# The third branch's two units ahead of the dilated one in each group of the first attention

## The reference

```python
# A: six query heads, one key head; the keys are picked by an index score
logits = einsum(q, k_picked) * scale;  p = softmax(logits);  o_a = p @ v_picked

# B: dilated, three groups of four heads, (window, dilation) = (128, 1), (512, 4), (2048, 16)
pos = t - dil * arange(window // dil + 1)
e = exp(logits - m);  den = sum(e);  o = (e / den) @ v
lse = m + log(den);   alpha = softmax over the three groups of lse
o_b = sum over the groups of alpha * o

# C: window of 128, eight query heads on two key heads, a sink per head
m = maximum(max(logits), sink);  den = sum(exp(logits - m)) + exp(sink - m)
o_c = (exp(logits - m) / den) @ v

merged = g0 * (o_a @ w_a) + g1 * (o_b @ w_b) + g2 * (o_c @ w_c)
```

## Time and profile before

| | |
|---|---|
| median of 3 runs | 3436.84 us |
| the profiled execution | 3435.26 us |
| its span | 3433.5 us |
| PE busy | 3325.6 us, 97% |
| PE weight loads busy | 2738.0 us, 80% |
| DVE busy | 1700.4 us, 50% |
| ACT busy | 1338.7 us, 39% |
| POOL busy | 950.7 us, 28% |
| mean granted clock of PE | 0.982 |

### The profile page before, as it was taken

How to read it: one execution, slowest core, us unless ns; L and a number is a source line. 1 busy time by engine, 2 the same in 40 slices (tenths; PEclk the granted TensorE clock), 3 DMA queues, 4 the chain that set the end, 5 groups by cost and what they waited for, 6 DMA issues and landing times. The chain is left out here.

```text
span 3433.5 us, 55220 instructions
## 1 busy us (share of the span) xinstructions
PE 3325.6 (97%) x22824; PEld 2738.0 (80%) x22824; DVE 1700.4 (50%) x2672; ACT 1338.7 (39%) x2039; POOL 950.7 (28%) x629
## 2 busy tenths in 40 slices
PE   8999999999999999999999999899999999899998
PEld 7777887888778778878887859888887758898887
DVE  5886334313259753451413665554444566454454
ACT  5646333323255543332324362343324353343322
POOL 3325002444443420034443341241101342141100
PEclk9999999999999999999999999999999999999999
DMA  4200222222221022222232100212222200112222
GB/s 157 80 20 28 105 104 88 98 94 103 86 99 62 1 80 104 103 86 98 98 114 103 62 1 4 100 50 95 90 97 105 86 1 4 66 49 102 94 97 74
DMA packets 59684, 264.93 MB, mean 77 GB/s; under 512 B 13248, under 2 KB 27968, under 8 KB 30528
## 3 DMA queue, kind: packets, MB, share of 16 engines
q1 hardware_dynamic: 59456, 261.65, 21.8%
HBM read 259.53 MB, written 2.10 MB: 76 GB/s over the span
## 5 line engine op out<-in xcount | busy, mean ns | idle before, releaser
L1491 POOL TENSOR_TENSOR w_lo_f<-raw_f,w_hi_f 128x2048 fp32r<-128x2048 f32 x60 | 275.7, 4595 | 382.0 <-ACT w_hi_f L390 382.0
L402 PE MATMUL ps<-u_hi,w_hi_d 128*128 128x512 f32 (+1 forms) x768 | 291.5, 380 | 6.8 <-POOL u_lo L2929 5.6
L403 PE MATMUL ps<-u_lo,w_hi_d 128*128 128x512 f32 (+1 forms) x768 | 287.3, 374 | 0.0
L404 PE MATMUL ps<-u_hi,w_lo_d 128*128 128x512 f32 (+1 forms) x768 | 287.3, 374 | 0.0
L390 ACT ACTIVATE w_hi_f<-raw_f 128x2048 fp32r<-128x2048 f32 x64 | 121.9, 1908 | 253.8 <-PE ps L404 243.8
L402 PE MATMUL ps<-hid_hi,w_hi_f 128*128 128x512 f32 x512 | 199.2, 389 | 0.0
L403 PE MATMUL ps<-hid_lo,w_hi_f 128*128 128x512 f32 x512 | 199.2, 389 | 0.0
L404 PE MATMUL ps<-hid_hi,w_lo_f 128*128 128x512 f32 x512 | 199.2, 389 | 0.0
L1518 DVE TENSOR_TENSOR hid<-hid 128x512 f32<-128x512 f32 x64 | 119.0, 1860 | 139.6 <-ACT hid L1467 137.8
L656 POOL TENSOR_TENSOR w_lo_a<-raw_a,w_hi_a 128x2048 fp32r<-128x2048 f32 x28 | 129.0, 4609 | 199.7 <-ACT w_hi_a L652 199.7
L402 PEld LDWEIGHTS ps<-u_hi,w_hi_d 128*128 128x128 f32 x768 | 146.6, 191 | 35.4 <-POOL u_lo L2929 7.2
(11 more groups left out here) (463 smaller groups left out, 8585.0 us busy)
## 6 DMA issues: line engine op xcount, KB each, us to landing
raw_d<-in_w SPq DMA_DIRECT2D x70, 1024.0 KB, 4.8
raw_f<-in_w SPq DMA_DIRECT2D x64, 1024.0 KB, 4.8
raw_c<-in_w SPq DMA_DIRECT2D x40, 1088.0 KB, 5.0
raw_a<-in_w SPq DMA_DIRECT2D x22, 1024.0 KB, 4.9
raw_p<-in_w SPq DMA_DIRECT2D x22, 1024.0 KB, 4.8
raw_a<-in_w SPq DMA_DIRECT2D x18, 512.0 KB, 4.9
wo_raw<-in_w SPq DMA_DIRECT2D x4, 1024.0 KB, 6.3
h<-in_x SPq DMA_DIRECT2D x8, 256.0 KB, 4.3
```

Of the source, the lines that this page charges most:

```text
L402: nc.tensor.matmul(out, w_hi, x_hi, start=start, stop=False)
L403: nc.tensor.matmul(out, w_hi, x_lo, start=False, stop=False)
L404: return nc.tensor.matmul(out, w_lo, x_hi, start=False, stop=stop)
L1491: nc.gpsimd.tensor_tensor(WF[2][:, k % 2, :], WF[0][:, k % 2, :], WF[1][:, k % 2, :].bitcast(F32), ALU.subtract).then_inc(S["w_lo"], 1)
```

## The change

The list `units` is put together in another order: in each of the eight groups the two C units come first, then the B unit, then the A units as before. All else is derived from the list, on every engine.

```diff
             units = []
             for i, unit in enumerate(b_units):
-                units += [unit, *c_units[2 * i:2 * i + 2], *a_units[3 * i // 2:3 * (i + 1) // 2]]
+                units += [*c_units[2 * i:2 * i + 2], unit, *a_units[3 * i // 2:3 * (i + 1) // 2]]
```

## The result

The changed kernel takes 3442.57 us (median of 20 runs, 3438.04 to 3445.92), the kernel before beside it 3435.69 us (median of 20, 3434.57 to 3439.12). The ratio is 1.0017 with a 95% interval of 1.0011 to 1.0023: slower by 3.8 to 7.9 us, by 5.8 in the middle. The forecast was 3434.1, in a range of 3430.5 to 3438.9. The profiled execution took 3444.3 us with a span of 3442.5; it was one of the longer ones. One execution of an experiment, `act_copy_late`, took 7471.31 us; it is a slow run that nothing here explains, and it is left out of that experiment's ratio.

The account below looks back on a forecast made before the run. PE's (TensorE's) summed work bounds the kernel, so only its stalls and low clock can pay. Per attention 0.9 + 0.4 - 0.25 + 0.3 = 1.35 us, for two 2.7: 3436.84 - 2.7 = 3434.1 us, range 3430.5 to 3438.9.

Parts of the forecast that it names:

- The start: First units of each attention: PE's one idle of 3.0 us becomes three short ones; 0.9 us gained, bounds 0 and 1.6.
- first rival: The clock stays low through the start, B0's turn all low: 0.9 us less gained per attention, 3435.9 us; chance 0.18.
- The stall at 245.43: PE's stall early in the stage, before a C unit's values, goes: 0.4 us gained per attention.
- new wait of 0.25 before the turn of B1: At B1, the chain from logits to `wide` outlasts PE's work between: about 0.25 us lost per attention.
- The stalls after short B steps: Stalls in the steps after B2, B4, B6: 1.00 and 0.56 stay, 0.3 left of 0.56; gain 0.3 us per attention.
- The queues: Attention's end: slab transfers come later, ACT waits 1.0 us, hidden from PE with 0.6 us to spare.
- third rival: Slab 3 us later than counted: ACT's wait delays C15's copy and last exponentials, 2.4 us per attention, 3438.9; chance 0.12.

Follow-up runs that it names:

- act_copy_late: Changed kernel with ACT's wait for the slab and its copy one step later, in step 36; 3434.3 us, ratio 0.9992 to before; again 3435.34, 0.9998.
- copies_first: Changed kernel with DVE copying the turned B7 out of PSUM ahead of `o_lo` in step 36; 3434.1 us, ratio 0.9996 to the kernel before.
- last_group_only: Kernel before with only the last of the eight groups in the new order; 3445.8 us, ratio 1.0024 to the kernel before.
- before_act_late: Kernel before, old order, with ACT's wait and copy of the slab moved to step 36; 3436.15 us, ratio 0.9999 to the kernel before.
- last_group_old: Changed kernel with the last group back in the old order, first seven groups in the new; 3436.58 us, ratio 0.9996 to the kernel before.
- before_late_fetch: Kernel before, old order, with SP's slab transfers held back until the logits of C15; 3437.12 us, ratio 1.0005 to the kernel before.

## Why the prediction was wrong

**The start: right in kind, too large.** The chain was close: I had the turn of C0 at 4.16 us after PE's start, it was at 4.33; that of C1 at 6.86, it was 6.78; that of B0 at 8.9, it was 8.84. The waits for `sc` are there:

```profile
232.83 0.69 PE L1009 MATMUL ps<-cst,sc 128*128 128x128 f32 x2 [1.10 <-POOL sc L1094]
...
235.28 0.69 PE L1009 MATMUL ps<-cst,sc 128*128 128x128 f32 x2 [1.04 <-POOL sc L1094]
...
237.34 4.35 PE L1006 MATMUL ps<-wide,sc 128*128 128x128 f32 x24
```

The clock was where I had it, or somewhat later; what I had wrong is the price of the turn. I let the clock come back 11.0 us after PE's start. In the first attention it came back at 240.3, 11.8 us after the start, and in the second at 1144.8, 11.2 after it, each time in the midst of the first dilated turn:

```profile
240.00:241.00 1.00, 1.00 (x10) 1.00 (x9) 0.31 (x2) 0.00 (x0) 0.00 (x0) 0.84 0.00 0
...
1136.00:1137.00 1.00, 1.00 (x12) 1.00 (x9) 0.81 (x4) 1.00 (x7) 0.32 (x1) 0.50 0.00 0
...
1139.00:1140.00 1.00, 0.34 (x4) 0.05 (x2) 0.46 (x5) 1.00 (x3) 0.86 (x2) 0.50 0.00 0
...
1143.00:1144.00 1.00, 1.00 (x7) 1.00 (x6) 0.69 (x5) 0.53 (x4) 0.40 (x1) 0.50 0.00 0
1144.00:1145.00 1.00, 1.00 (x7) 1.00 (x6) 0.46 (x1) 0.63 (x4) 0.00 (x0) 0.58 0.00 0
```

The turn took 4.28 and 4.01 us where I had 3.6. I had priced a record at low clock at 0.187 us, 4.50 divided by 24. But the turn of before began and ended at full clock. In its trace records start 0.213 us apart at low clock and 0.112 at full. In the second attention the 10 or 11 records at low clock are what I had forecast, and their price with a first record of 0.37 us makes the difference; in the first attention some 3 more records were at low clock.

So the first rival was not the account of these two starts, since it had the whole turn at low clock. It is that of three starts in the experiments. In both of `copies_first` and in the first of `act_copy_late` the clock came back 13.8 to 14.1 us after PE's start, and the turn took 5.2 to 5.4 us:

```profile
236.64 5.43 PE L1006 MATMUL ps<-wide,sc 128*128 128x128 f32 x24
```

Its price was wrong with the same 4.50: such a start does not come out even, it takes 0.6 us more than the mean of the old order, 13.9. The rule of the Trainium skill named with this rival (TensorE: Matmul & The Clock Gate, "A second HAM failure mode: psum-queue depth-cycling") has the clock go down and up between bursts. These rows agree with it only in part: the bursts did run at low clock, but from 1134.6 to 1144.8 it did not come up once. Twelve starts with the new order are on record in six profiles: nine take 13.0 to 13.5 us, three 14.5 to 14.6, against 13.6 to 14.1 converted of the eight with the old order. The gain is 0.3 us in the mean, not 0.9.

**The stall at 245.43: wrong.** It came again, as 0.42 before the values of C2, with the same releaser. The new wait of 0.25 before the turn of B1 did not come. These two errors of mine nearly cancel.

```profile
248.57 0.44 PE L1030 MATMUL ps<-pt,cv 128*64 128x128 f32 x4 [0.42 <-DVE o_lo L1147]
...
249.57 2.94 PE L1006 MATMUL ps<-wide,sc 128*128 128x128 f32 x24
```

**The stalls after short B steps: right.** They moved from the C to the A units: 1.00 at B2 (258.33 to 259.97 where 0.64 is the work), 0.57 at B4, and 0.15 at B6 where I had 0.3. These lines answer to the earlier trace rows:

```profile
258.33 0.70 PE L975 MATMUL ps<-qk 64*128 64x256 f32 x2
259.35 0.70 PE L975 MATMUL ps<-qk 64*128 64x256 f32 x2 [0.32 <-DVE o_lo L1147]
259.97 0.66 PE L1009 MATMUL ps<-cst,sc 128*128 128x128 f32 x4
...
285.08 1.49 PE L975 MATMUL ps<-qk 64*128 64x384 f32 x4
```

**The queues: the step that failed.** "So it is hidden with 0.6 us to spare; the cover is the turn of B7." I had seen that the slab comes late and that ACT waits for it ahead of the copy of C15, and I had followed this one copy to PE: it does cost only 0.23 us. I had not gone through the rest of what stands behind ACT's wait: the exponentials and then `o_hi` of unit 31 in step 36, for which DVE waits, with the copies of B7 behind. "The last masks, scalings by DVE and copies come after that turn and keep their distance" is the sentence in which this is lost; the copies of B7 kept no distance. In the old order no B unit is turned in step 36, so there was nothing in the rows of before that showed this wait; but the code has it: `o_lo` stands ahead of the copies. The size was off too. The wait was 2.14 and 1.45 us, not 1.0, since the transfers took 8.0 and 7.3 us from the end of their issue instead of 7.0. And I had no term for the low clock after a new rest, 1.6 of the 4.2 us in the first attention.

This was my third rival. It had the right place, but at 3438.9 its price was 3.7 us short of the measured time, it went by another path than I gave, and I gave it a chance of 0.12, on the ground that the slab's own time had no reason to grow. The path needed no such reason: 3.6 us of lateness had used up 3.4 of cover.

## What to carry to other kernels

When a unit is moved behind others, go through what waits for its last reader, here a transfer into its place, and then list everything in order behind the instruction that will wait, on its own engine and on each engine that waits for that one, until the list reaches the bound engine; one item followed to its end is not enough. A wait that has had microseconds of cover may sit ahead of work that it has nothing to do with; when the cover goes, put it behind that work first, which took away here the whole loss (`act_copy_late`: 0.9992 and 0.9998 of before). And a rest of PE costs more than its length if the clock falls behind it, here 1.6 us on top of 2.3.

## What the runs showed of the hardware that I had not expected

The clock fell to 1.2 GHz behind a rest of 2.27 us (first attention of the changed kernel, 2.28 in its second profile) and did not behind one of 1.88 us (second attention, 1.81 in the second profile). The length alone does not decide it: in the second attention of `last_group_only` PE stood for 0.51 us and, 1.7 us of work later, for 2.27, and the clock stayed at 1.00; in the first attention, with rests of 1.41 and 2.28 us, it fell. What decides was not tried.

In seven of the twelve starts with the new order the clock stayed at 0.50 for 10.2 us through the short bursts, in the second attention of the changed kernel from 1134.6 to 1144.8 us, though PE was busy for a good part of that. In the other five, and in all eight of the old order, it came up once in between. So one and the same start can cost 13.0 or 14.6 us.

The two transfers of the slab took 6.8 to 7.0 us from the end of their issue in the kernel before, in `before_act_late` and in `last_group_old`. When issued later, with the last group in the new order, they took 7.9 to 8.3 us in the first attention and 7.2 to 7.4 in the second, and 8.1 and 8.5 in `before_late_fetch`. No other transfer of a like size is in the trace at that time; what makes the difference was not tried.
